# A two-layer decoder trunk on one Trainium2 core: the MLPs' up products of groups two to eight as seven products of quarters

## The reference

```python
h = rms_norm(x, norm_mlp_g[layer])
x = x + jnp.square(jax.nn.relu(h @ mlp_w_up[layer])) @ mlp_w_down[layer]
```

## Time and profile before

| | |
|---|---|
| median of 3 runs | 2515.63 us |
| profiled execution | 2515.74 us, span 2514.0 us |
| granted TensorE clock, mean over the span | 0.986 of full |
| busy share of the span | PE 95%, PEld 77%, DVE 64%, ACT 42%, POOL 52% |
| DMA | 140.88 MB, mean 56 GB/s |
| MLP of layer 0 / layer 1, by the span's time | about 789 to 1460 us / 1854 to 2514 us |

### The profile page before, as it was taken

The page is one execution under the profiler, slowest core; times in us unless marked ns, Lnnn a source line. Parts: engine busy times, 40 slices in busy tenths (PEclk is TensorE's granted clock), DMA queues, the critical chain, the costliest instruction groups (busy, mean ns, idle before and its releaser), DMA issues.

```text
span 2514.0 us, 31082 instructions
## 1 busy us (share of the span) xinstructions
PE 2399.8 (95%) x11073; PEld 1937.6 (77%) x11073; DVE 1613.8 (64%) x2338; ACT 1059.6 (42%) x1821; POOL 1302.4 (52%) x684
## 2 busy tenths in 40 slices
PE   8889997898899999999999999979899999999999
PEld 6778875557888888888888877857787888888887
DVE  6889878988865654456448556676555644565483
ACT  4556887766545232232222356254442322222210
POOL 3212325998853664566549231164346654665490
PEclk9999998999999999999999999989999999999999
DMA  5321131004001211121112221230112111211121
GB/s 160 89 50 39 51 84 43 1 18 135 18 18 51 68 51 33 50 67 58 33 42 67 76 89 42 68 109 14 51 34 67 59 33 42 67 59 40 35 67 67
DMA packets 165306, 140.88 MB, mean 56 GB/s; under 512 B 24457, under 2 KB 136146, under 8 KB 165202
## 3 DMA queue, kind: packets, MB, share of 16 engines
q1 hardware_dynamic: 158738, 132.98, 17.8%
q10 hardware_dynamic: 6464, 6.56, 0.9%
HBM read 116.17 MB, written 13.63 MB: 52 GB/s over the span
## 4 chain that ended last, share of the span: by engine, by line
PE 70%; DVE 13%; ACT 6%; issue 5%; POOL 4%; DMA 1%; SPq 0%; ACTq 0%; DVEq 0%
PE ps L2534 21%; PE ps L2536 21%; PE ps L2535 21%; ACT signs L1464 3%; POOL PL L1017 2%; POOL cl L1059 1%; PE ps L2527 1%; DVE ub L2421 1%; DVE ps L2158 1%; DVE ps L2056 1%; DVE score L1933 1%; DVE shared L2418 1%; PE ps L3055 1%; DVE acc L2365 0%; PE ps L2776 0%
## 5 line engine op out<-in xcount | busy, mean ns | idle before, releaser
L2534 PE MATMUL ps<-h_hi,w_hi 128*128 128x512 f32 x1672 | 660.2, 395 | 0.0
L2536 PE MATMUL ps<-h_hi,w_lo 128*128 128x512 f32 x1672 | 652.6, 390 | 0.0
L2535 PE MATMUL ps<-h_lo,w_hi 128*128 128x512 f32 x1672 | 652.4, 390 | 0.0
L843 POOL TENSOR_TENSOR w_lo<-w_raw,w_hi 128x1024 fp32r<-128x1024 f32 x69 | 183.1, 2654 | 353.0 <-ACT w_hi L1487 348.6
L2536 PEld LDWEIGHTS ps<-h_hi,w_lo 128*128 128x128 f32 x1672 | 314.7, 188 | 66.6
L2534 PEld LDWEIGHTS ps<-h_hi,w_hi 128*128 128x128 f32 x1672 | 314.9, 188 | 65.3 <-issue 2.4
L2535 PEld LDWEIGHTS ps<-h_lo,w_hi 128*128 128x128 f32 x1672 | 315.0, 188 | 64.8 <-issue 1.9
L2418 DVE TENSOR_TENSOR x_res<-ps,x_res 128x1024 f32<-128x1024 f32 x224 | 268.7, 1221 | 115.3 <-PE ps L2536 115.3
L861 POOL TENSOR_TENSOR w_lo<-w_raw,w_hi 128x1024 fp32r<-128x1024 f32 x112 | 267.7, 2406 | 127.1 <-ACT w_hi L1349 89.9
L2399 DVE TENSOR_TENSOR u_all<-ps,u_all 128x512 f32<-128x512 f32 x112 | 77.1, 690 | 381.1 <-ACT u_all L1360 381.1
L2534 PE MATMUL ps<-w_hi,uo_hi 128*128 128x512 f32 x784 | 307.8, 393 | 6.0 <-DVE shared L2418 3.6
(11 more groups left out here) (397 smaller groups left out, 4451.6 us busy)
## 6 DMA issues: line engine op xcount, KB each, us to landing
w_raw<-in_mlp_w_up SPq DMA_DIRECT2D x64, 512.0 KB, 4.0
w_raw<-in_mlp_w_down SPq DMA_DIRECT2D x64, 512.0 KB, 3.6
w_raw<-in_even_w_in SPq DMA_DIRECT2D x23, 512.0 KB, 3.9
x_res<-in_x SPq DMA_DIRECT2D x16, 512.0 KB, 8.2
t<-xg SPq DMA_DIRECT2D x120, 64.0 KB, 2.0
w_raw<-in_odd_w_in SPq DMA_DIRECT2D x10, 512.0 KB, 4.0
scr_x<-x_res SPq DMA_DIRECT2D x8, 512.0 KB, 2.6
x_res<-scr_x SPq DMA_DIRECT2D x8, 512.0 KB, 4.5
```

The lines of the kernel that those rows point to most:

```text
L843: g.tensor_tensor(w_lo[:, k, :], w_raw[:, n % 2, :], w_hi[:, k, :].bitcast(F32), ALU.subtract).then_inc(w_ready, 1)
L2534: t_.matmul(out_, ah, bh, start=first, stop=False)
L2535: t_.matmul(out_, ah, bl, start=False, stop=False)
L2536: return t_.matmul(out_, al, bh, start=False, stop=last)
```

## The change

Group one keeps its up part of eight products. For groups two to eight the up part becomes seven products of quarters. The two halves of the k-tiles by the two halves of the tokens give four quarters of h; the seven products use them alone or combined.

- **Combinations of h.** At the end of group one's up part TensorE multiplies h_hi and h_lo with a plus or a minus identity (`combine`): 16 banks of 512 columns, 8 of them with 4 matmuls and 8 with 2. ScalarE copies each bank to h_hi, VectorE makes h_lo from the bank and h_hi. TensorE waits for the last of these before the first down product.
- **Streaming.** The combinations overwrite all four quarters of h_hi and h_lo. Three quarters of h are saved to DRAM first, in six pieces numbered 0 to 5 (12 DMAs of 512 KB), and in each of groups two to eight the pieces are loaded again into the operand buffers uo_hi/uo_lo while these are free (12 DMAs of 512 KB a group). The first, fourth and sixth up product use them; the other four use the combinations.
- **Sums in PSUM.** The seven products add up in four pairs of banks X, Y, V, Z; ScalarE copies X to Y and Y to Z inside PSUM and V to `ub`; VectorE adds `ub` to Y and Z. Relu and square then run over a quarter, 1024 elements a partition.
- **Weights.** Up weights come as quarters; GpSimd makes four sums of them and splits seven quarters in place of four. Down weights get four sums and seven splits as before, in another order. The low parts of all seven u operands are now VectorE's.
- **Group eight** has the new up part and keeps the plain down product; its square and split are VectorE's and ScalarE's by quarters.

The diff, cut to its core (a first column of 12 blanks is taken off):

```diff
+        S_ORDER = (1, 0, 2, 3, 4, 5, 6)
+        FIRST_SLOTS, S_SLOTS = (0, 4, 1, 2, 3, 1, 4), (3, 4, 2, 0, 1, 3, 4)
+        UP_SLOTS = (0, 2, 1, 3, 4, 0, 1)
+        BANK_X, BANK_Y, BANK_V, BANK_Z = 0, 2, 4, 6
+        S_BANKS = (BANK_V, BANK_X, BANK_Y, BANK_Z) * 3 + (BANK_V, BANK_Z)
         S_UP = ((1, 0), (2, 0), (3, 0), (0, 0), (0, 1), (1, 1), (2, 1), (3, 1))
-        S_OPERAND = (0, 1, 2, 0, 1, 2, 0)
+        S_OPERAND = (0, 1, 2, 1, 0, 2, 1)
+        LOW_COUNT = (1, 2, 3, 5, 5, 6, 7)
...
+            sp.wait_ge(w_ready, first + up_order(layer, True).index(r) + 1)
+            load_down(0, r)
+        sp.wait_ge(n_lo, 32 * layer + 32)
+        for b, (k0, c) in enumerate(((0, 1), (4, 0), (4, 1))):
+            for m in range(2):
+                for o, t in enumerate((h_hi, h_lo)):
+                    sp.dma_start(scr_h[:, (0, 4, 2)[b] + m, 2 * o:2 * o + 2, :],
+                                 t[:, k0 + 2 * m:k0 + 2 * m + 2, c * HT:(c + 1) * HT].bitcast(F32)).then_inc(dram_saved, 16)
...
+    def stream(piece, o, to):
+        for m, t in enumerate(to):
+            sp.dma_start(t[:].bitcast(F32), scr_h[:, piece, 2 * m:2 * m + 2, :]).then_inc(stream_landed[o], 16)
...
+        sp.wait_ge(dram_saved, 16 * (12 + (12 + T) * layer))
+        for piece, o, e in ((0, 0, 4), (1, 2, 5), (2, 1, 6)):
+            sp.wait_ge(down_done, S_SUMS * i + (g0 - S_SUMS + 4 * (e + 1)))
+            stream(piece, o, (uo_hi[o], uo_lo[o]))
+        sp.wait_ge(up_done, ups + 1)
+        stream(3, 0, (uo_hi[0], uo_lo[0]))
+        stream(4, 2, (uo_hi[2], uo_lo[2]))
+        if last:
+            sp.wait_ge(quarters_done, quarter_base(layer, i) + SHARED_FREE)
+            sp.wait_ge(stream_landed[1], 64 * i + (64 * S_ITERS * layer - 32))
+            stream(5, 1, (late_hi, late_lo))
+            return
+        for r, n in ((1, 5), (0, 6), (2, 6), (3, 7)):
+            sp.wait_ge(w_ready, before + n)
+            load_down(i, r)
+        sp.wait_ge(up_done, ups + 4)
+        stream(5, 1, (uo_hi[1], uo_lo[1]))
+    first_group()
     with sp.Fori(1, S_ITERS) as i:
         group(i)
...
+    def group(i, last=False):
+        before, ups = units_before(layer, i), up_base(layer, i)
+        sums, downs = 8 * i + (s0 - 4), S_SUMS * i + (g0 - S_SUMS)
+        def up_landed(r):
+            pool.wait_ge(raw_landed[r], 32 * i + (l0[r] + 16))
+        low(before + 1, UP_SLOTS[0], raws[0])
+        up_landed(2)
+        up_landed(3)
+        pool.wait_ge(down_done, downs + 16)
+        s1 = fp32(UP_SLOTS[1])
+        summed(s1, raws[2], raws[3], ALU.add)
+        up_landed(0)
+        pool.wait_ge(sums_ready, sums + 1)
+        summed(raws[2], raws[0], raws[2])
+        pool.wait_ge(sums_ready, sums + 2)
+        pool.wait_ge(w_ready, before + 1)
+        summed(raws[0], raws[0], s1)
+        pool.wait_ge(sums_ready, sums + 3)
+        low(before + 2, UP_SLOTS[1], s1)
+        low(before + 3, UP_SLOTS[2], raws[0])
+        low(before + 4, UP_SLOTS[3], raws[1])
+        pool.wait_ge(w_ready, before + 4)
+        summed(raws[0], raws[1], raws[0], ALU.add)
+        low(before + 5, UP_SLOTS[4], raws[2])
+        low(before + 6, UP_SLOTS[5], raws[0])
+        if last:
+            low(before + 7, UP_SLOTS[6], raws[3])
+            return
+        def down_landed(r):
             pool.wait_ge(raw_landed[r], 32 * i + (l0[r] + 32))
...
+        d1, d0, d2 = (fp32(k) for k in S_SLOTS[:3])
+        down_landed(2)
+        down_landed(0)
+        summed(raws[2], raws[2], raws[0])
+        low(before + 7, UP_SLOTS[6], raws[3])
+        down_landed(3)
+        pool.wait_ge(sums_ready, sums + 5)
+        pool.wait_ge(up_done, ups + 2)
+        summed(d2, raws[3], raws[2])
+        down_landed(1)
+        pool.wait_ge(sums_ready, sums + 6)
+        pool.wait_ge(up_done, ups + 4)
+        summed(d1, raws[1], d2)
+        pool.wait_ge(up_done, ups + 5)
+        summed(d0, d2, raws[0])
+        pool.wait_ge(sums_ready, sums + 8)
+        down_lows(before + 7, S_SLOTS)
+    first_group()
     with pool.Fori(1, S_ITERS) as i:
         group(i)
...
+    group(S_ITERS, True)
+    for n in range(n0 + MLP_UNITS - 4, n0 + MLP_UNITS):
...
+    def late_operands(i, slots):
+        act.wait_ge(raw_landed[2], 32 * i + (l0[2] + 32))
+        sums_at(i, 0)
+        if slots is FIRST_SLOTS:
+            sums_at(i, 2)
+        weights(slots[5], raws[2])
+        operand(4, quarter(0, 1))
+        act.wait_ge(raw_landed[3], 32 * i + (l0[3] + 32))
+        sums_at(i, 1)
+        weights(slots[6], raws[3])
+        operand(3, quarter(0, 0))
+        sums_at(i, 2)
+        operand(5, quarter(1, 0))
+        act.wait_ge(u_squared, 4 * i + (q0 + 4))
+        sums_at(i, 3)
+        operand(6, ub[:])
...
+        act.wait_ge(up_done, up_base(layer, 1) - 16 + c + 1)
+        bank = COMB_BANKS[c]
+        if c == 0:
+            act.wait_ge(dram_saved, 16 * (12 + (12 + T) * layer))
+        s.activation(h_hi[place], ps[:, bank, :], ACT.Copy).then_inc(products_read, 1)
...
+        operand(1, uo_sum[:])
+        relu(6)
+        act.wait_ge(u_squared, q0 + 2)
+        operand(2, ub[:])
+        act.wait_ge(sums_ready, s0 + 4)
+        weights(FIRST_SLOTS[0], fp32(FIRST_SLOTS[0]))
+        relu(7)
+        weights(FIRST_SLOTS[1], fp32(FIRST_SLOTS[1]))
+        weights(FIRST_SLOTS[2], fp32(FIRST_SLOTS[2]))
+        for c in range(16):
...
+        act.wait_ge(quarters_done, quarters + C22_DONE)
+        operand(0, quarter(1, 1))
+        act.wait_ge(sums_ready, sums + 8)
+        weights(S_SLOTS[1], fp32(S_SLOTS[1]))
+        weights(S_SLOTS[2], fp32(S_SLOTS[2]))
+        product_done(6)
+        positive(BANK_Y, 1, 0)
+        act.wait_ge(raw_landed[0], 32 * i + (l0[0] + 32))
+        weights(S_SLOTS[3], raws[0])
         act.wait_ge(u_squared, 4 * i + (q0 + 1))
...
+        operand(1, uo_sum[:])
+        product_done(7)
+        positive(BANK_Z, 0, 1)
+        act.wait_ge(raw_landed[1], 32 * i + (l0[1] + 32))
+        weights(S_SLOTS[4], raws[1])
         act.wait_ge(u_squared, 4 * i + (q0 + 2))
         operand(2, ub[:])
...
+        act.wait_ge(quarters_done, quarters + C21_DONE)
+        late_operands(i, S_SLOTS)
     act.wait_ge(down_done, g0)
...
+    first_group()
     with act.Fori(1, S_ITERS) as i:
...
+    def downs(i):
+        for e, k in enumerate(S_ORDER):
+            for t in (0, 2):
+                dve.wait_ge(down_done, S_SUMS * i + (g0 + 4 * e + t + 2))
+                earlier = [n for n in range(e) if set(S_TARGETS[S_ORDER[n]]) & set(S_TARGETS[k])]
+                if earlier:
+                    dve.wait_ge(x_added, S_SUMS * i + (g0 + 4 * earlier[-1] + t + 2))
+                for c in S_TARGETS[k]:
+                    dst = shared[:, t:t + 2, :] if c is None else                                     x[:, 4 * (1 - c[0]) + t:4 * (1 - c[0]) + t + 2, c[1] * HT:(c[1] + 1) * HT]
+                    bank = S_BANKS[2 * e + t // 2]
+                    ins = v.tensor_tensor(dst, ps[:, bank:bank + 2, :], dst, ALU.add)
+                ins.then_inc(x_added, 2)
+            if e == 0:
+                v.tensor_tensor(ub[:], quarter(0, 1), ub[:], ALU.subtract).then_inc(u_squared, 1)
+                low(i, 4, 4, quarter(0, 1))
+            if e == 1:
+                low(i, 5, 3, quarter(0, 0))
+            if e == 2:
+                low(i, 6, 5, quarter(1, 0))
+            if e == 3:
+                summed(i, 4)
+                low(i, 7, 6, ub[:])
...
+        if n == 0:
+            v.tensor_tensor(s3, quarter(0, 0), quarter(1, 0), ALU.subtract).then_inc(u_squared, 1)
+            summed(i, 1)
+        if n == 1:
+            v.tensor_tensor(ub[:], quarter(1, 1), s3, ALU.subtract).then_inc(u_squared, 1)
+            v.tensor_tensor(quarter(1, 0), quarter(1, 0), quarter(1, 1), ALU.add).then_inc(u_squared, 1)
+            summed(i, 3)
...
+                operands(0, 1)
+                low(0, 2, 1, s3)
+        low(0, 3, 2, ub[:])
+        for c in range(16):
+            dve.wait_ge(products_read, first_reads(layer) + 8 + c + 1)
+            place = COMB_PLACES[c]
...
+                v.tensor_tensor(u_lo[:, part[0], part[1]], of(r, c), u_hi[:, part[0], part[1]].bitcast(F32),
+                                ALU.subtract).then_inc(u_ready, 1)
+        dve.wait_ge(products_read, copies + Y_COPIED)
+        y = ps[:, BANK_Y:BANK_Y + 2, :]
+        v.tensor_tensor(y, y, ub[:], ALU.add).then_inc(quarters_done, 1)
+        squared(C11_POSITIVE, BANK_X, 0, 0)
+        last_low(1, 0, 0)
+        dve.wait_ge(up_done, ups + 5)
+        v.tensor_tensor(of(1, 1), ps[:, BANK_Z:BANK_Z + 2, :], ub[:], ALU.add).then_inc(quarters_done, 1)
+        dve.wait_ge(quarters_done, quarters + Z_READ)
+        v.scalar_tensor_tensor(out=of(1, 1), in0=of(1, 1), scalar=0.0, in1=of(1, 1), op0=ALU.max, op1=ALU.mult) \
+            .then_inc(quarters_done, 1)
+        if not last:
+            low(i, 1, 0, quarter(1, 1))
+        last_low(2, 1, 1)
+        squared(C12_POSITIVE, BANK_Y, 1, 0)
```

(64 more changed lines are left out.)

499 lines of the change are left out of this document (275 added, 224 removed).

## The result

The changed kernel takes 2649.03 us (median of 4 runs, 2644.74 to 2654.17) against 2516.37 us for the kernel before (4 runs, 2515.26 to 2521.07): a ratio of 1.0523, 95% interval 1.0506 to 1.0540. The profiled execution took 2644.74 us (span 2643.0, mean granted clock 0.957; before 0.986).

The account below looks back on a forecast made before the run. PE was taken to bound the kernel, each MLP group being a full train of matmuls. Per layer 25.5 (group one) + 41 (groups two to seven) + 0 (group eight) = 66.5, both 133 on 2515.7: 2649 us, range 2535 to 2720.

Parts of the forecast that it names:

- Matmuls: MLP groups of the new form: 336 matmuls, 76.2 us without PE waits; group one's combinations 10.9 us, rests +2.5.
- The chain: Groups two to seven, from T (end of seventh up product): second operand low part at T + 15.9, stall 10.5 us.
- Turns: VectorE operations reading SBUF alone take 1.2 us alone, up to 3.3 behind a GpSimd operation.
- With no turn taken: Bound for groups two to seven: four SBUF operations at 1.2 us each, low part 5.4 us earlier, stall of 5.
- Clock: After a stall, 0 to 3.5 us lost, 1.7 taken; sign: granted clock near 0.97 in MLP windows.
- A group: Groups two to seven: 76.2 + 10.5 + 1.7 = 88.4 us against 81.6, +6.8 each.
- group one: +25.5 us a layer: matmuls +10.9, rests +2.5, stall of 10.4 before the fourth down product, clock 1.7.
- group eight: Matmuls -5.4 us, a stall of 4 for GpSimd's split, clock 1 to 2: 0 net.
- Costed at nothing: ACT's copies inside PSUM, DVE's adds onto PSUM (nearest 1.0 to 1.2 us) and stream pieces 0 to 4: hidden.
- Turns don't matter: Rival: POOL idle during DVE's chain, stall near 5 shrinking to 3, no clock loss: 2524 us; chance 0.09.
- The DMA queue as the bound: Rival: transfers of 2.6 rather than 1.5 us, some 9 us more in twelve groups: 2757 us; chance 0.09.
- Faster, with every operand in time: Rival: down operands ready under the first down product, 2487 us; with no wait at all 2461; chance 0.10.

Follow-up runs that it names:

- the second version: Changed kernel plus six edits: VectorE's order, group one's slots, GpSimd's wait, fourth operand split before fifth, earlier relu, earlier up low part: 2478.16 us.
- the five edits that were tried singly: Each alone in the changed kernel: VectorE's order 2659.89 us, earlier relu 2626.90, group one's slots 2624.83, GpSimd's wait 2593.08, earlier up low part 2629.36.
- the swap: ScalarE and VectorE split the fourth down operand before the fifth, ub's difference later; never run alone; the second version without it takes 2558.50 us.
- the six: The five edits that were tried singly and the swap, all in the changed kernel, which makes the second version: 2478.16 us.

## Why the prediction was right

The forecast was 2649, the median is 2649.03. To the last us this is luck: the forecast adds 133 us, and the profiled execution, from which the steps are read, took 2644.74, 129 more than the one before. But the steps hold too:

- **Matmuls.** 336 in a group, 76.2 us without a wait: the second version comes to 77.2 with 0.7 us of wait. The 48 of the combinations are where they were put: their first starts at 824.54, the first down product at 838.16, 13.6 us later, 10.9 and 2.7 for the rest (2.5 taken).
- **The chain.** Forecast and measured, from T: r2 landed T - 19.9, T - 20.4; GpSimd's low part T - 15.1, T - 15.6; r3 T - 11.3, T - 11.5; sums T - 3.1, T - 3.4; square of the sixth quarter T + 1.1, T + 0.8; uo_sum T + 3.6, T + 3.4; relu of the seventh T + 5.6, T + 5.4; low part T + 15.9, T + 15.6. Each is 0.2 to 0.5 us early, a difference that arises at r2 and is carried through. Stall 10.5, measured 9.94 (10.45 for 10.4 in group one): the low part comes 0.3 us earlier, and the first down product ends at T + 5.8, not T + 5.4.
- **Turns.** The 2.5, 3.3 and 3.3 us put on ub, the sum in place and the low part, after the earlier trace rows, were 2.47, 3.37 and 3.15, and the run in which GpSimd waits shows 1.22 for each. The Trainium skill's page "SBUF — State Buffer", section "SBUF: two separate sides", has the shared port pair held for the whole instruction. The trace agrees: GpSimd's operation of 1012.20 and the next end at 1017.75, and uo_sum, begun at 1016.29, ends 1.1 us after that. What the forecast worked out from the rule, 1.2 + 2.4 = 3.6 us for every operation, was too long. VectorE waits only for what is left of GpSimd's operation: 2.47 and 2.54 us where it comes in the middle of one, and 3.43 at most in the first MLP of any run.
- **One bound.** "With no turn taken" the forecast has the low part 5.4 us earlier, for four operations of 1.2 us each. Its own terms give (2.5 + 2.5 + 3.3 + 3.3) - 4 x 1.2 = 6.8 us and a stall of 3.7; 5.4 is what three of them give, and the run in which GpSimd waits frees just three: 5.35. The range of 2580 to 2715 doesn't follow from its terms either, which give 2569 to 2706. Neither changes the forecast.
- **Clock.** 1.7 us a stall taken. Measured: the down part of a group is 1065.93 - 1015.53 = 50.4 us; less 168 x 0.227 = 38.1, less the wait of 9.94 and some 0.4 of ordinary gaps (the down part of the second version: 39.1 with 0.7 of wait), 2.0 us are left. Eight matmuls start 0.43 us behind the one before. A sign that the forecast gave was off: it had a granted clock near 0.97 in the MLP windows, and it is 0.94. The clock falls within the wait, where it costs nothing: it is 0.50 (last section) from 1026 us on, and the matmuls come back at 1031.19.
- **A group** grew by 6.5 us for 6.8 forecast; group one by 24.9 for 25.5; group eight by 0.4 for 0, with GpSimd's split 3.65 us late for 4. The start-to-start distance of groups before is 82.24, where the prediction took 81.6, and after it is 88.73, where it had 88.4: both too short, so the difference held.
- **Costed at nothing.** The copy inside PSUM, a form not seen before, takes 1.01 us. VectorE waits for it, but PE never waits for VectorE's addition behind it:

```profile
1437.38 1.01 ACT L1590 ACTIVATE ps<-ps 128x1024 f32<-128x1024 f32 x1 [4.05 <-PE ps L2981]
```

- **The rivals.** "Turns don't matter" gave 2524. With most of the turns taken out of the chain (GpSimd waiting) the time is 2593: the stall is 4.6 us, near the 5 at which this rival starts, but it doesn't shrink to 3, and the clock loss stays. So the turns are 56 us of the 125 by which it was wrong. The DMA queue as the bound: down loads land in 5.2 us and not 3.6, yet PE itself waits for no load in the MLP (GpSimd does, 6.7 and 4.1 us a group), and the second version moves 136 GB/s in a group with 0.7 us of wait. "Faster, with every operand in time" was wrong for this code, and other code comes near it: the second version has no long stall in group one either, so its 2478 goes with that rival's 2461 for no wait at all. Of the 17 us between them twelve groups of 77.2 for 76.2 are 12.

What the prediction did not see is how many links lie close behind the one it worked out. It followed the chain to the second down product; the runs show that the fourth and fifth operands' low parts come next, and hide behind it. So the five edits that were tried singly range from 11 us lost to 56 gained, and with the swap, which frees the next link, the six gain 171.

## What to carry to other kernels

When a change thins out the engine that bounds, write down for every operand when it is due and when its chain ends, with the durations the operations have in each other's company, not alone. Two engines that take turns at one access are best kept apart in time where one of them is on the path: a wait on the engine that has slack bought 56 us here. And test edits of an order in groups as well as singly, since one that loses alone may gain once the next link is out of the way.
